# Float32r index scores with signs, paired key transposes and an earlier start, in a one-core hybrid decoder step

## The reference, cut to what matters

```python
def indexer_scores(qi, wi, ki):            # qi (8,4,16,64), wi (8,4,16), ki (8,4100,64)
    s = jax.nn.relu(jnp.einsum('bthd,bsd->bths', qi, ki).astype(jnp.float32))
    return jnp.einsum('bths,bth->bts', s, wi.astype(jnp.float32))

ki_past = cache_kidx[layer, page_table].reshape(DB, n_pages * PAGE_SIZE, D_IDX)
ki_all = jnp.concatenate([ki_past, ki_new], axis=1)
sc = jnp.where(adm, indexer_scores(qi, wi, ki_all), -jnp.inf)
_, idx = lax.top_k(sc, topk)               # 256 of 4100
```

## Time and profile before

| what | value |
|---|---|
| median of 3 runs | 3245.47 us (3240.72 to 3249.15) |
| the profiled execution | 3247.65 us, of which its span 3245.9 us |
| PE busy | 2994.7 us, 92% of the span |
| DVE, ACT, POOL busy | 2325.7, 1180.1, 689.4 us |
| granted TensorE clock, mean | 0.95 |

### The profile page before, as it was taken

How to read it: one execution, slowest core, us unless ns; L and a number is a source line. 1 busy time by engine, 2 the same in 40 slices (tenths; PEclk the granted TensorE clock), 3 DMA queues, 4 the chain that set the end, 5 groups by cost and what they waited for, 6 DMA issues and landing times. The chain is left out here.

```text
span 3245.9 us, 50979 instructions
## 1 busy us (share of the span) xinstructions
PE 2994.7 (92%) x20721; PEld 2751.9 (85%) x20721; DVE 2325.7 (72%) x3011; ACT 1180.1 (36%) x1736; POOL 689.4 (21%) x509
## 2 busy tenths in 40 slices
PE   7978999999997488876997899999999999999999
PEld 6944888999875478854887799999999999999998
DVE  6025994699643666546785788898888888888887
ACT  4223112222453511133322455555555433333332
POOL 4344333467351134232332000000000000000000
PEclk9999999999998689877998999999999999999999
DMA  5423233469684100046334356666666965555552
GB/s 183 120 74 89 88 100 96 134 187 284 204 267 163 51 1 1 1 126 191 107 116 148 115 157 190 201 192 190 193 187 192 337 213 191 184 189 191 196 173 101
DMA packets 501704, 496.87 MB, mean 153 GB/s; under 512 B 33418, under 2 KB 437738, under 8 KB 499829
## 3 DMA queue, kind: packets, MB, share of 16 engines
q1 hardware_dynamic: 465136, 423.39, 42.7%
q0 software_dynamic: 13440, 42.02, 4.2%
q10 hardware_dynamic: 22896, 28.20, 2.5%
HBM read 379.57 MB, written 115.20 MB: 152 GB/s over the span
## 5 line engine op out<-in xcount | busy, mean ns | idle before, releaser
L3709 ACT ACTIVATE om_ring<-om_raw 128x1024 fp32r<-128x1024 f32 x456 | 482.5, 1059 | 601.1 <-PE om_ps L3489 392.4
L3472 PE MATMUL om_ps<-om_hc,om_ring 128*128 128x272 f32 x5376 | 682.8, 290 | 9.1 <-DVE om_ring L3521 5.4
L3472 PEld LDWEIGHTS om_ps<-om_hc,om_ring 128*128 128x128 f32 x5376 | 682.1, 190 | 10.1 <-DVE om_ring L3521 6.2
L3489 PE MATMUL om_ps<-om_hc,om_ring 128*128 128x272 f32 x5376 | 681.0, 290 | 6.3 <-issue 4.4
L3489 PEld LDWEIGHTS om_ps<-om_hc,om_ring 128*128 128x128 f32 x5376 | 679.7, 189 | 7.6 <-issue 5.7
L3521 DVE TENSOR_TENSOR om_ring<-om_raw,om_ring 128x1024 fp32r<-128x1024 f32 x456 | 554.8, 1222 | 131.4 <-ACT om_ring L3709 131.2
L523 PE MATMUL pm_ps<-h,w_ring 128*128 128x280 f32 x2688 | 356.5, 294 | 8.3 <-issue 7.8
L523 PEld LDWEIGHTS pm_ps<-h,w_ring 128*128 128x128 f32 x2688 | 350.3, 190 | 14.3 <-issue 14.2
L470 POOL TENSOR_TENSOR w_ring<-w_raw,w_ring 128x1024 fp32r<-128x1024 f32 (+2 forms) x110 | 251.1, 2303 | 342.1 <-ACT w_ring L556 341.9
L541 PE MATMUL pm_ps<-w_ring,h 128*128 128x512 f32 (+2 forms) x1152 | 237.2, 365 | 8.0 <-POOL w_ring L470 8.0
L541 PEld LDWEIGHTS pm_ps<-w_ring,h 128*128 128x128 f32 x1152 | 200.0, 189 | 41.6 <-issue 8.0
(11 more groups left out here) (572 smaller groups left out, 4035.0 us busy)
## 6 DMA issues: line engine op xcount, KB each, us to landing
om_raw<-in_w_up SPq DMA_DIRECT2D x128, 512.0 KB, 4.9
om_raw<-in_w_down SPq DMA_DIRECT2D x128, 512.0 KB, 5.2
hid_scratch<-om_x SPq DMA_DIRECT2D x64, 952.0 KB, 7.4
om_hc<-hid_scratch SPq DMA_DIRECT2D x56, 1088.0 KB, 11.8
w_raw<-in_w_in SPq DMA_DIRECT2D x112, 512.0 KB, 4.0
ao_raw<-in_w_out SPq DMA_DIRECT2D x32, 384.0 KB, 3.6
as_qb<-q_rows SPq DMA_DIRECT2D x32, 256.0 KB, 4.8
om_x<-xT_scratch SPq DMA_DIRECT2D x7, 1088.0 KB, 11.5
```

The costliest lines, as they stand in the source:

```text
L3472: last = pe.matmul(ps[:, bank_of(q, idx), 0:HM], f32r(ring[:, n % SLOTS, a, P * k:P * (k + 1)]), f32r(hc[:, c, b, k, :]), start=(idx in (0 ...
L3489: last = pe.matmul(ps[:, bank_of(q, idx) + i, 0:HM], w, f32r(hc[:, slot, b, GJ * half + j, :]), start=(idx in (0, 1, 3) and j == a == b == 0),
L3709: act.activation(f32r(ring[:, n % SLOTS, 0, :]), source(n), ACT.Copy).then_inc(hi, 1)
```

## The change

- The units are cut anew: 4 groups of 1024 keys by 8 sequences, still 32. A unit is one gather of 128 rows of 2 KB (8 keys). Two neighbouring keys of 64 features fill a column of 128, so PE transposes straight from `raw`, and ACT's `lay` is gone.
- Transposed keys are kept in two float32r parts, `kiT` high by ACT from PSUM and low by DVE. The query operand has two parts too. score is three float32r matmuls of 512 columns.
- |wi| is multiplied into the queries, so that the relu's result only has to be summed with the signs of wi. The relu's result is kept in two float32r parts (high by ACT, low by a DVE scalar_tensor_tensor), and `add` is two float32r matmuls with the signs, which float32r holds exactly.
- The operands and the first four gathers are made in the `pi` block (class `SampleKeys`): fetches on SP at loads 5 and 7, small DVE work, 16 transposes on PE behind load 8 and one float32 matmul of 512 columns behind load 9, four gathers at the end of POOL's program. The last load of `pi` computes its second half of tokens first, and ACT copies the last two heads' queries from `pi_stage` with four DMAs. ACT doesn't wait for the stores at the end of `pi`, but in the next block.
- The new keys are scored at the start of the scores block and not at its end (24 matmuls with 2 columns, later 16 more).
- The first two loads of `pm` are fetched and split within the scores block: ACT's highs behind the relus of units 9, 11, 19 and 21, POOL's lows between its gathers.

```diff
@@ project_in
-        ps = [... for n in range(banks)]
+        if after:
+            after.use_bank(ps[-1])
+            banks -= 1
...
+            if after:
+                after.queries(sp, staged_until[N - 1])
...
+                if turned_round(n):                       # the last load of pi
+                    for x in range(2):
+                        y = half_out(n, x)                # 1, then 0
+                        for k in range(KT):
+                            for a, z in ((0, 0), (0, 1), (1, 0)):
+                                ins = pe.matmul(bank_of(b + x)[:, 0:HALF], piece(a, k), f32r(h[:, z, k, two_halves(y)]), ...)
+                        ins.then_inc(product, 1)
...
+                    if turned_round(n) and x == 0:
+                        after.last_queries(act, stage[:, at % 4, 0:cols])
@@ class SampleKeys
+    def sync(self, sp, n):
+        if n == 5:                                        # 8 page-table pieces, c_mod, c_rows, c_toks
...
+        if n == 7:
+            sp.wait_ge(self.stored[0], 32)                # then the new keys (2) and the head weights
...
+    def queries(self, sp, staged):
+        for n in range(4):
+            sp.wait_ge(self.stored[n], 16 * ((staged - n + 3) // 4))
+        src = self.dram["projT"][0:(HI - 2) * DI, TP:TOK].rearrange("(h d) t -> d h t", d=DI)
+        for x in range(2):
+            sp.dma_start(self.qs[DI * x:DI * (x + 1), 0:HI - 2, :], src).then_inc(self.s["q_in"], 16)
...
+    def vector(self, dve):                                # ends with
+        for heads, done, count in ((slice(0, HI - 2), "q_in", 32), (slice(HI - 2, HI), "last_q_in", 64)):
+            dve.wait_ge(s[done], count)
+            for x in range(2):
+                half = slice(DI * x, DI * (x + 1))
+                last = dve.tensor_tensor(self.q[half, :, x, heads], q4[half, :, heads], size_of[half, :, heads], ALU.mult)
+            step(last)
+        step(dve.tensor_copy(f32r(self.q_parts[:, 0]), self.q))
+        dve.tensor_tensor(f32r(self.q_parts[:, 1]), self.q, self.q_parts[:, 0], ALU.subtract)
...
+    def gpsimd(self, pool):
+        pool.wait_ge(self.s["offs_ready"], 1)
+        for m in range(self.GR):
+            self.gather(pool, m)
@@ sample_scores
+            for m in range(GR, U):                        # POOL
+                pool.wait_ge(s["turned"], m - GR + 1)
+                keys.gather(pool, m)
+                for (n, part), unit in AT_HIGHS.items():  # {(0, 0): 9, (0, 1): 11, (1, 0): 19, (1, 1): 21}
+                    if unit == m - GR:
+                        low(n, part)
...
-                act.activation(laid[:, n % 2], raw[:, n % GR].rearrange("p x (r d) -> p r x d", r=4), ACT.Copy
+                act.activation(f32r(kiT[:, n % 2, 0, :]).rearrange("p (r q) -> p r q", r=4), t_ps[n % 2][:, :, :], ACT.Copy
...
-                act.activation(relu[:, n % 2, :], s_ps[n % 2][:, :], ACT.Relu)
+                act.activation(f32r(relu[:, n % 2, 0, :]), s_ps[n % 2][:, :], ACT.Relu).then_inc(s["r_hi"], 1)
...
-                dve.tensor_copy(kiT[:, n % 2, :] ..., t_ps[n % 2] ...)
+            def k_low(n):
+                dve.wait_ge(s["k_hi"], n + 1)
+                dve.tensor_tensor(f32r(kiT[:, n % 2, 1, :]) ..., t_ps[n % 2][:, :, :], kiT[:, n % 2, 0, :] ..., ALU.subtract)
+            for n in range(U):
+                if n + 1 < U:
+                    k_low(n + 1)
+                dve.wait_ge(s["r_hi"], n + 1)
+                dve.scalar_tensor_tensor(out=f32r(relu[:, n % 2, 1, :]), in0=s_ps[n % 2][:, :], scalar=0.0,
+                                         in1=relu[:, n % 2, 0, :], op0=ALU.max, op1=ALU.subtract).then_inc(s["r_lo"], 1)
+                if n >= DB and n % DB in (2, 4):
+                    scores_out(n // DB - 1, n % DB // 2 - 1)
...
-                pe.matmul(s_ps[n % 2][:, :], qbd[:, p] ..., kiT[:, n % 2, :], start=True, stop=True)
+                k = [f32r(kiT[:, n % 2, a, :]) for a in range(2)]
+                pe.matmul(s_ps[n % 2][:, :], stacked(0, b), k[0], start=True, stop=False)
+                pe.matmul(s_ps[n % 2][:, :], stacked(1, b), k[0], start=False, stop=False)
+                pe.wait_ge(s["k_lo"], n + 1)
+                pe.matmul(s_ps[n % 2][:, :], stacked(0, b), k[1], start=False, stop=True).then_inc(s["scored"], 1)
...
-                pe.matmul(c_ps[g % 2][:, :], w[:, p] ..., relu[:, n % 2, :], start=(p == 0), stop=(p == 3))
+                pe.matmul(c_ps[g % 2][:, :], summing(b), f32r(relu[:, n % 2, 0, :]), start=(b == 0), stop=False)
+                pe.wait_ge(s["r_lo"], n + 1)
+                pe.matmul(c_ps[g % 2][:, :], summing(b), f32r(relu[:, n % 2, 1, :]), start=False, stop=(b == DB - 1))
@@ build
-            project_in(nc, dram, sb, plan[3:], "pm", 4, side=ChooseThenAttend(nc, dram, consts, sb),
+            project_in(nc, dram, sb, plan[3:], "pm", 4, weights=weights, fetched=2, side=ChooseThenAttend(nc, dram, consts, sb),
```

More of the change, by code:

```diff
@@ L637, in _ @@
             for n in range(4 if front else 1, N):
-                if not low_on_dve(n):
+                if not low_on_dve(n) and n >= fetched:
                     low(pool, n)
@@ L2510, in sample_scores @@
+def sample_scores(nc, dram, consts, sb, keys, weights, loads):
     with ExitStack() as ctx:
@@ new lines, in w_high @@
+            def w_high(n, part):
+                act.wait_ge(weights.raw_in[part], 16 * sum(len(ld.segs) for ld in loads[:n + 1]))
+                act.activation(f32r(ring[:, n, 0, half_of_load(part, loads[n])]), w_raw[:, part, whole_of_load(loads[n])], ACT.Copy
+                               ).then_inc(weights.hi_ready[part], 1)
+            k_high(0)
+            for n in range(U):
+                if n == 0:
+                    act.wait_ge(s["own_scored"], 1)
+                    act.activation(f32r(own[:, 0, :]), own_ps[:, 0:TS // 2], ACT.Relu).then_inc(s["own_hi"], 1)
+                if n + 1 < U:
+                    k_high(n + 1)
@@ L2656, in add @@
[L2656 to L2661 removed]
+                    pe.wait_ge(s["r_lo"], n - 1)
+                pe.wait_ge(s["k_hi"], n + 1)
+                k = [f32r(kiT[:, n % 2, a, :]) for a in range(2)]
@@ new lines, in own_scores, with own_sums @@
+            def own_scores():
+                u = DT // 2
+                for b in range(DB):
+                    for a, z in ((0, 0), (1, 0), (0, 1)):
+                        last = pe.matmul(own_ps[:, u * b:u * (b + 1)], stacked(a, b), f32r(keys.knT[:, z, b, :]),
+                                         start=(a == z == 0), stop=(z == 1))
+                last.then_inc(s["own_scored"], 1)
+            def own_sums():
+                u = DT // 2
+                pe.wait_ge(s["own_lo"], 1)
+                for b in range(DB):
+                    for a in range(2):
+                        last = pe.matmul(own_ps[0:2 * TS, 256:256 + u], summing(b), f32r(own[:, a, u * b:u * (b + 1)]),
+                                         start=(b == a == 0), stop=(b == DB - 1 and a == 1))
+                last.then_inc(s["own_summed"], 1)
@@ L2683, in _ @@
-            last.then_inc(s["summed"], 1)
+            add(U - 1, *units[U - 1])
 class Choose:
```

394 lines of the change are left out of this document (239 added, 155 removed).

## The result

The changed kernel took 3203.59 us (median of 4 runs, 3197.14 to 3213.65) against 3247.31 us (4 runs) for the kernel before: a ratio of 0.9862, 95% interval 0.984 to 0.9884, 43.7 us faster. The forecast was 3206 us, in a range of 3194 to 3219.

The account below looks back on a forecast made before the run. The old scores' loop was bound by a ring of PE, relu and `lay`, 2.72 us a unit; the new by DVE, by a hair. Terms sum to 90.8 us against 130.1, gain 39.3, so 3206 us, range 3194 to 3219.

Parts of the forecast that it names:

- work beside `pi`: In the first projection: 16 small transposes 1.9 us and a float32 matmul 0.96 on PE, +2.9 us; other engines' work covered.
- first border: Between `pi` and the scores: one eviction 0.40, one issue 0.33, the border 0.3; 1.1 us, no wait for stores.
- loop, own sums, stalls, last sums: Scores block: 32 units at 1.75 us, 56.0; own sums 1.3; stalls 8; relu, `r_lo`, second sum and waits 1.6.
- end of block: After the scores' last sum: two `scores_out` and the border, 1.8 us; the new keys' tail is gone.
- first pm load: Start of pm: 60 matmuls 13.9 us plus 0.8 lost to the clock after PE idles some 3 us; 14.7.
- The stalls: In the scores' loop: gathers 14 and 16, then another pair, wait behind POOL's lows; 8 us, range 0 to 14.
- Given back later?: Later stages: DVE's slack of 16.3 us is over twice 7.7 us, so the whole gain stays; without it 7.7 would go.
- loop slower: Rival, scores' loop: semaphore latencies between ACT, DVE and PE make 2.1 to 2.5 us a unit, 3217 to 3230 us; chance 0.12.
- clock, period of 3.28: Rival, scores' loop: PE's clock falls to 1.2 GHz, 3.28 us a unit, 3255 us; chance 0.04 together with gathers.
- doesn't gather faster: Rival, scores' loop: landings of 11 us for doubled gathers would reach 2.98 us a unit; chance 0.04 together with clock.
- lead of PE lost: Rival, in pm: DVE or SP late at load 20 or 23, 3214 us; no chance of its own, within other ranges.
- No stalls, loop on PE: Rival, scores' loop: 1.64 us a unit with stalls of 0 to 2 us, 3195 down to 3193 us; chance 0.08.

Follow-up runs that it names:

- no early weights: Changed kernel with no load of pm fetched or split in the scores block, pm fetching its first two loads itself: 3203.8 us, ratio 0.9858 to the kernel before.
- float32 products: Changed kernel with score and add as one float32 matmul each, without low parts of keys and relu: 3212.5 us, ratio 0.9893 to the kernel before.
- late splits: Changed kernel with only pm's first load split early, POOL's lows behind its last gather: 3187.7 and 3191.0 us, ratios 0.9810 and 0.9866 to the kernel before.

## Why the prediction was right, point by point

The prediction's sum from 188.15 us on, term by term, against the profiled execution of the changed kernel:

| term | predicted | measured | from |
|---|---|---|---|
| work beside `pi` | 2.9 | 2.0 | 190.19 - 188.15 |
| first border | 1.1 | 2.0 | 190.19 to 192.16 |
| start of block | 3.4 | 3.2 | 192.16 to the next turn, 195.36 |
| loop, own sums, stalls, last sums | 66.9 | 66.7 | 195.36 to 262.06 |
| end of block | 1.8 | 2.7 | 262.06 to 264.76 |
| first pm load | 14.7 | 16.5 | 264.76 to 281.24 |
| sum | 90.8 | 93.1 | gain 37.0, against 39.3 |

In the other two profiles of the changed kernel the gain was 40.0 and 38.3. The mechanism was right: a loop near PE's own work, a first border in place of the long one, and stalls behind POOL's lows. That the sum came within 2.3 us is in part luck, since terms that were too long (the loop, the stalls) paid for one that wasn't there (the clock in the loop). That the whole kernel's median came within 2.4 us of the forecast is in part luck too: of the profiled pair's 47.5 us only 37.0 lie in the stretch.

- *Work beside `pi`.* Mis-sized, 2.1 us in the trace for 2.9: the 16 transposes of 32x32 and 2x2 took 1.08 us together, where those of 128x128 had priced them at 1.9. The 2.0 of the table is the difference of two executions.
- *The loop.* Right in sum, wrong in its bound. "DVE is the longest by a hair" failed: `r_lo` took 0.69 us and not 0.75, its gaps and copies don't fall in every unit, and it was 82% busy where over 90% was forecast. The unit is PE's, 1.59 to 1.61 where PE alone had been put at 1.64: transposes 0.36 and not 0.49, first score matmul 0.31 and not 0.23. That makes 51.5 us and not 56.0, and the stalls were 4.2 us shorter than their term. Most of it was taken back by two things that the sum didn't have. The clock: windows of 8.44, 11 and 12 us at 0.80, 0.84 and 0.86 miss 1.7 + 1.8 + 1.7 = 5.2 us of full clock (an estimate from these windows). "The clock at 0.98 or more in the loop" was wrong, it was 0.93 from 195.36 to 262.06. And short waits of PE for DVE and ACT, 2.4 us over the loop.
- *`scores_out`.* Mis-sized: 0.68 predicted, 1.11 measured. The row of before wrote 512 adjacent elements; the new one writes every eighth. By the code the output's stride is all that tells the two copies apart; no run varies it alone. In the loop PE waits 0.2 to 0.55 us at a group's copies, and at the end the two take 2.16 us for 1.36, 0.8 of the 0.9 us by which that term missed.
- *The stalls.* The mechanism was right in place and kind, turn 14 with 2.34 us (2.0 predicted). Turn 16 lost 0.28, not 1.4. Turn 24 lost 1.18 and turn 26 nothing here, 1.35 and 1.33 in the other two profiles. The waits of the turns for gathers add up to 3.8 us here, 5.2 and 5.1 in the other two; the term was 8, 6.8 by its own count of the gathers. Taking POOL's lows from between the gathers took the stalls away, which shows their cause.
- *The first border.* The prediction said that a late operand chain would delay it by as much; it did, by 0.9. The four issues took 0.9 us each and not 0.43, so the last two heads' queries landed at 189.4.
- *POOL beside DVE.* No cost, as said. The lines by form, 196 to 262 us:

```profile
L2807 DVE SCALAR_TENSOR_TENSOR ss_relu<-ss_s,ss_relu 128x512 fp32r<-128x512 f32 x32 | 22.0, 688 | 3.9 <-ACT ss_relu L2768 3.1 <-issue 0.6
L2779 DVE TENSOR_TENSOR ss_kiT<-ss_t,ss_kiT 128x512 fp32r<-128x512 f32 x31 | 21.3, 688 | 12.7 <-ACT ss_kiT L2750 11.2 <-issue 1.4
...
L2786 DVE COPY sm_ssc_all<-ss_c 32x512 f32<-32x512 f32 x6 | 6.8, 1128 | 0.1
L2734 POOL TENSOR_TENSOR w_ring<-w_raw,w_ring 128x1024 fp32r<-128x1024 f32 x4 | 9.5, 2380 | 5.6 <-ACT w_ring L2755 5.5
```

  The two splits with one input in PSUM keep 0.69 us on average over all units, those beside POOL's four lows included. The lows take 2.38 us, as against 2.36 before. The Trainium skill (SBUF — State Buffer, Who interferes with whom) says that a DVE instruction with at most one input in SBUF doesn't contend with GpSimd; the trace agrees.
- *The first pm load.* The clock cost 2.6 us and not 0.8. I had scaled the loss before the change by the length of the stop, 3 us for 8. That rule fails at both ends: stops of 7.98 and 10.03 us (kernel before, no early weights) went with loads of 15.5 us, one of 2.7 with 15.5 to 16.5 in the changed kernel, and one of 2.66 with 13.95 after the float32 products.
- *Given back later?* No: by the first matmul of the convolution's own strips the gain was still 36.0 us (1042.73 against 1006.71), so DVE's slack held.
- *What the sum could not have.* The profiled pair differs by 47.5 us: 37.0 in the stretch, 6.7 in the scan stage, 3.8 in all else. The medians differ by 43.7 to 52. Against the stretch's 37 to 40 this leaves 4 to 14 us outside the stretch, where the code is the same. The scan stage's clock can make them, since it moves one and the same kernel by as much; that it did in the runs without a profile isn't shown, and the 3.8 are open.

The rivals: "loop slower", "clock, period of 3.28" and "doesn't gather faster" fell by the unit of 1.61, "lead of PE lost" by the 36.0 us that were still there at 1006.71. "No stalls, loop on PE" described the late splits: its forecast, 3195, stands beside their 3187.7 and 3191.0.

## What to carry to other kernels

When a loop gets short, look again at what sits between its transfers: a 2.4 us job in the queue that issues gathers was free at 2.45 us a unit (the float32 products) and stopped TensorE at 1.6. Put such jobs behind the last gather. Price each copy by its output's stride and each DMA issue by its own form, and check at a border which engine's last instruction is the late one: here one of its two copies given to another engine took 1 us off DVE's last work. Before believing a few microseconds, cut the span at landmarks: here a stage that nobody touched took 260 or 274 us in executions of one kernel.

## What the runs showed of the hardware

- TensorE's granted clock can fall while it is busy: to 0.57 behind the first border with a stop of only 0.30 us ahead and PE busy all the while, behind 24 matmuls of 2 columns; whether these are the cause no run tests. Which level follows isn't steady: the same instructions ran at 0.80 over 8.4 us in the changed kernel and at 0.50 over 12.9 us with the late splits.
- Behind a stop of 2.7 us the first load, 60 matmuls, took 15.4 to 16.5 us with its first 4 us at a clock of 0.50 to 0.61, in six profiles; with the stop cut to 0.75 or 0.45 us it took 13.95 to 14.0. But with the same stop of 2.66 us behind the loop of float32 products it took 13.95 too, at 1.00 throughout.
- In the scan stage the clock follows one of a few patterns: 260, 261, 268, 270 or 274 us for the same instructions, 260 four times within 0.3 us and 274 five times within 0.7, in twelve profiles.
- A copy of 32x512 from PSUM took DVE 0.68 us into adjacent elements and 1.11 us into every eighth; ACT took 1.17 for the latter.
- ACT's issue of a transfer of 64 partitions by 32 columns from SBUF to SBUF took 0.9 us, that of its store of a whole strip 0.33 to 0.60.
